# Expert outputs: from a table of rows gathered at the end to weighted rows scattered onto the output with accumulation

## What is computed

```python
# h: (1, 512, 1024); 4 groups of 4 experts, 256 hidden units each
pg_top, g_idx = lax.top_k(p_g, 1)                   # one group for each token
pe_top, e_idx = lax.top_k(p_e, 2)                   # two experts of that group
wts = pg_top * pe_top / sum(pe_top)
combine = sum(one_hot(eid, 16) * wts)
a = einsum('bsd,edf->bsef', h, w_gate)
u = einsum('bsd,edf->bsef', h, w_up)
hid = silu(a) * u * combine
out = x1 + einsum('bsef,efd->bsd', hid, w_down)
```

## Time and profile before

| What | us |
|---|---|
| median of 3 runs | 579.16 |
| lowest and highest run | 576.29, 579.25 |
| the profiled execution, device time | 577.23 |
| its span in the trace | 575.5 |
| PE busy in the span | 498.2 |
| first transposes of expert tile 0 start | 378.0 |
| last product of tile 12 ends | 541.9 |
| last row gathered back lands | 567.8 |

### The profile page before, as it was taken

One profiled execution on the slowest core, in us unless ns is written; L12 is line 12 of the kernel. 1 busy time (PEld: TensorE's weight loads), 2 busy tenths in 40 slices (PEclk: granted clock), 3 DMA queues, 4 the chain that ended last, 5 costly groups with the idle time before them and its releaser, 6 DMA issues.

```text
span 575.5 us, 7543 instructions
## 1 busy us (share of the span) xinstructions
PE 498.2 (87%) x2858; PEld 262.2 (46%) x2858; DVE 232.8 (40%) x591; ACT 112.0 (19%) x273; POOL 134.7 (23%) x150
## 2 busy tenths in 40 slices
PE   5898899999989999999999969369999999999600
PEld 3553544445656676655666655323333333333100
DVE  1127345505697534544455653333421122211133
ACT  2200332233213343313223220300000001000100
POOL 2211388732899100000010211303100000000050
PEclk9999899999998999999999967559999999999955
DMA  8999910006000000470002493636999999970165
GB/s 303 422 386 420 422 56 0 1 1 235 1 1 1 0 1 2 183 329 1 0 1 71 160 354 105 241 110 202 338 419 423 424 425 423 427 303 38 76 235 209
DMA packets 21501, 111.53 MB, mean 194 GB/s; under 512 B 3152, under 2 KB 4688, under 8 KB 16720
## 3 DMA queue, kind: packets, MB, share of 16 engines
q1 hardware_dynamic: 13680, 88.68, 38.5%
q10 hardware_dynamic: 4320, 13.83, 6.1%
q0 software_dynamic: 3456, 8.39, 4.1%
HBM read 81.53 MB, written 33.55 MB: 200 GB/s over the span
## 4 chain that ended last, share of the span: by engine, by line
PE 74%; DVE 7%; issue 4%; DMA 3%; ACT 1%; POOL 1%; POOLq 1%; DVEq 0%; ACTq 0%
PE bank L1416 17%; PE bank L1164 12%; PE bank L1302 10%; PE bank L1437 8%; PE bank L1139 7%; PE bank L1226 5%; PE bank L1240 4%; PE bank L1267 3%; PE bank L1199 3%; PE bank L1401 2%; DMA arena<-expert_rows,small 2%; PE bank L1254 1%; POOL arena L575 1%; PE bank L1424 1%; PE bank L1316 1%
## 5 line engine op out<-in xcount | busy, mean ns | idle before, releaser
L1164 PE MATMUL bank<-arena 128*128 128x512 f32 (+1 forms) x256 | 115.2, 589 | 5.5 <-DVE arena L783 3.1
L1416 PE MATMUL bank<-arena 128*32 128x512 f32 x832 | 96.3, 608 | 1.4 <-DVE arena L1074 0.8
L1139 PE MATMUL bank<-arena 128*128 128x128 f32 (+1 forms) x412 | 61.0, 284 | 20.8 <-DVE arena L865 4.6
L1164 PEld LDWEIGHTS bank<-arena 128*128 128x128 f32 x256 | 49.6, 196 | 61.4 <-issue 54.6
L1139 PEld LDWEIGHTS bank<-arena 128*128 128x128 f32 (+1 forms) x412 | 50.2, 144 | 56.9 <-issue 42.8
L1302 PE MATMUL bank<-arena 128*128 128x512 f32 x128 | 63.5, 624 | 0.0
L1416 PEld LDWEIGHTS bank<-arena 128*32 128x32 f32 x832 | 27.0, 112 | 61.4 <-issue 59.9
L865 DVE COPY arena<-bank 128x512 f32<-128x512 f32 (+2 forms) x64 | 36.2, 586 | 35.7 <-PE bank L1139 35.7
L1437 PE MATMUL bank<-arena 128*32 128x512 f32 x416 | 47.4, 595 | 0.8 <-DVE arena L1090 0.8
L575 POOL DMA_INDIRECT arena<-expert_rows,small x8 | 8.4, 1053 | 144.8 <-issue 144.8
L457 POOL TENSOR_SCALAR small<-small 128x1 f32<-128x1 f32 x16 | 3.7, 232 | 157.5 <-ACT arena L638 95.8
(11 more groups left out here) (148 smaller groups left out, 506.3 us busy)
## 6 DMA issues: line engine op xcount, KB each, us to landing
arena<-in_w_gu SPq DMA_DIRECT2D x17, 2048.0 KB, 13.8
arena<-in_w_dn SPq DMA_DIRECT2D x17, 1024.0 KB, 13.8
slot_rows<-arena SPq DMA_DIRECT2D x1, 11264.0 KB, 36.3
arena<-slot_rows ACTq DMA_DIRECT2D x13, 512.0 KB, 9.5
expert_rows<-arena ACTq DMA_DIRECT2D x13, 512.0 KB, 10.1
expert_rows<-arena SPq DMA_DIRECT2D x1, 4608.0 KB, 45.5
arena<-in_w_out SPq DMA_DIRECT2D x2, 2048.0 KB, 8.2
arena<-in_x SPq DMA_DIRECT2D x4, 512.0 KB, 10.8
```

What stands on the lines that cost most here:

```text
L1139: last = nc.tensor.transpose(TPB[p % 2][0:s.shape[-1], b * P:(b + 1) * P], s, ident)
L1164: last = nc.tensor.matmul(product_bank(i)[:, 0:width], hT[:, k, t * P:(t + 1) * P], w[:, k, :], start=(k == 0), stop=(k == KD - 1))
L1416: last = nc.tensor.matmul(GU[g % 2][BLK * b:BLK * (b + 1), :], xT[g % 2][:, k, BLK * b:BLK * (b + 1)], w_gu[n % RING][:, k, :], start=(k = ...
```

## The change

`expert_rows`, `y_back`, the gathers and the additions on DVE are gone. Instead SP stores x1 to the output (four DMAs, right behind the load of gate and up of the fifth expert in the ring), and each expert tile's rows are added to the output in DRAM by indirect DMAs that accumulate (`compute_op=ALU.add`), issued by POOL (`add`). A tile holds rows of two experts, and a token may have chosen both, so a tile is added in two runs: run 0 takes the rows of the tile's first expert, run 1 those of its second; rows of the other run and empty slots get a row number far out of bounds and are left out. POOL waits for a run to land (`added`) before it issues the run of another expert of the same group. Two runs of the same expert (run 1 of a tile, run 0 of the next) are issued together. Between groups nothing is waited for, as no token has experts of two groups. `y_sb` has three buffers.

The rows must be weighted before they are added. So each slot gets a tag of two numbers, the token's row number and its weight, in a small DRAM table `slot_tags`: filled with the out-of-bounds number early (in place of the fill of `expert_rows`), written by indirect DMAs of 8 bytes a row from POOL beside the rows themselves (eight early ones on the first slots, eight on the final slots), and read back by ACT (`load_tags`, 12 tiles, later the overflow tiles). `left_y` and `right_y` multiply by the weight as they copy. DVE makes the two lists of row numbers from the tags (`tag_rows`). The weights are needed earlier: ACT's exponentials and DVE's `weights_out` move up into the routing of each token tile.

```diff
+        def added_before(g):
+            return 16 * sum(2 if i < ITEMS else 1 for i in range(g % 3, g, 3))
...
-            sp.dma_start(y_dram[(ITEMS + 1) * P:, :].rearrange("(r p) d -> p r d", p=P),
-                         zero.unsqueeze(1).to_broadcast([P, EXTRA - 1, D_MODEL])).then_inc(s_zero, 16)
+            sp.wait_ge(s_fill, 1)
+            sp.dma_start(tag_dram.rearrange("(p r) c -> p (r c)", p=P), tag_fill).then_inc(s_zero, 16)
...
             sp.wait_ge(s_y, len(groups))
             load_gu(4, 4)
+            for t in range(T):
+                sp.wait_ge(s_x1, group["b", t, 1] + 1)
+                sp.dma_start(out[t], x_sb[:, t, :]).then_inc(s_out, 16)
...
-            for t in range(T):
-                sp.wait_ge(s_fin, t + 1)
-                sp.dma_start(out[t], x_sb[:, t, :]).then_inc(s_out, 16)
             sp.wait_ge(s_out, 16 * T)
...
+            def dispatch_tags(t, of, done, rows):
+                for k in range(TOP):
+                    nc.gpsimd.indirect_dma_start(
+                        out=tag_dram, out_offset=bass.IndirectOffsetOnAxis(ap=of[:, t, k:k + 1], axis=0),
+                        in_=tags[:, t, k, :], in_offset=None,
+                        bounds_check=rows * P - 1, oob_is_err=False).then_inc(done, 16)
+
+            def early_tags(t):
+                pool.wait_ge(s_wts, t + 1)
+                dispatch_tags(t, slots[0], s_tagged, ITEMS)
...
             dispatch(0)
             x1_root(2)
+            early_tags(0)
             out_root(1, 3)
             dispatch(1)
+            early_tags(1)
             x1_root(3)
             dispatch(2)
             dispatch(3)
+            early_tags(2)
+            early_tags(3)
...
-            for par in range(2):
-                pool.wait_ge(s_yst[par], 16 * ((LAST + 2 - par) // 2))
+                dispatch_tags(t, slots[1], s_over, TILES)
+
+            pool.wait_ge(s_out, 16 * T)
+
+            def add(g, run):
+                pool.wait_ge(s_ya, g + 1)
+                pool.wait_ge(s_yv, g + 1)
+                pool.wait_ge(s_tok, 1 if g < ITEMS else 2)
+                nc.gpsimd.indirect_dma_start(
+                    out=out_rows, out_offset=bass.IndirectOffsetOnAxis(ap=tag_row[:, run, g:g + 1], axis=0),
+                    in_=y_sb[g % 3], in_offset=None,
+                    bounds_check=SEQ - 1, oob_is_err=False, compute_op=ALU.add).then_inc(s_add[g % 3], 16)
+
+            def added(g, run):
+                pool.wait_ge(s_add[g % 3], added_before(g) + 16 * (run + 1))
+
+            for g in range(0, ITEMS, 3):
+                add(g, 0)
+                added(g, 0)
+                add(g, 1)
+                add(g + 1, 0)
+                added(g, 1)
+                added(g + 1, 0)
+                add(g + 1, 1)
+                add(g + 2, 0)
+                added(g + 1, 1)
+                added(g + 2, 0)
+                add(g + 2, 1)
+            added(LAST - 1, 1)
+            add(LAST, 0)
...
-            for t in range(T):
-                for k in range(TOP):
-                    nc.gpsimd.indirect_dma_start(
-                        out=y_back[t][k], out_offset=None, in_=y_dram,
-                        in_offset=bass.IndirectOffsetOnAxis(ap=slots[2][:, t, k:k + 1], axis=0),
-                        bounds_check=(ITEMS + EXTRA) * P - 1, oob_is_err=False).then_inc(s_back[t], 16)
+            added(LAST, 0)
...
+            act.wait_ge(s_tagged, 16 * TOP * T)
+            load_tags(0, ITEMS)
+
             def left_y(g):
                 act.wait_ge(s_dn, 2 * g + 1)
-                if g >= 2:
-                    act.wait_ge(s_yst[g % 2], 16 * (g // 2))
-                nc.scalar.copy(y_sb[g % 2][:, 0:512], YR[g % 2][0][:, :]).then_inc(s_ya, 1)
+                act.wait_ge(s_tag, 16 if g < ITEMS else 32)
+                if g >= 3:
+                    act.wait_ge(s_add[g % 3], added_before(g))
+                nc.scalar.activation(y_sb[g % 3][:, 0:512], YR[g % 2][0][:, :], ACT.Copy,
+                                     scale=tag_sb[:, g, 1:2]).then_inc(s_ya, 1)
...
                     if g + 3 == LAST:
-                        act.wait_ge(s_over, 16 * TOP * T)
+                        act.wait_ge(s_over, 2 * 16 * TOP * T)
+                        load_tags(ITEMS, TILES)
                     load_x(g + 3)
...
             dve.wait_ge(s_k, 16)
+            for k in range(TOP):
+                link(nc.vector.tensor_copy(tags[:, :, k, 0], konst[:, K_ROW:K_ROW + T]))
...
                 if s in RANKS_AT:
                     ranks_out(RANKS_AT[s])
+                    weights_out(RANKS_AT[s])
...
             ranks_out(2)
+            weights_out(2)
             logits_out(T - 1)
             ranks_out(T - 1)
+            weights_out(T - 1)
...
-            for t in range(T):
-                dve.wait_ge(s_back[t], 32)
-                for k in range(TOP):
-                    ins = nc.vector.scalar_tensor_tensor(x_sb[:, t, :], y_back[t][k], wts[:, t, k:k + 1],
-                                                         x_sb[:, t, :], ALU.mult, ALU.add)
```

More of the change, by code:

```diff
@@ L130, in build @@
         hidT = [at(144, 2, P), at(145, 2, P)]
-        y_sb = [at(110, D_MODEL), at(114, D_MODEL)]
-        y_back = [[at(kb + 4 * i, D_MODEL) for i in (0, 1)] for kb in (16, 24, 48, 56)]
+        y_sb = [at(110, D_MODEL), at(114, D_MODEL), at(136, D_MODEL)]
         route = at(118, T, P)
@@ L166, in build @@
         logits = sm(T, E)
-        wts = sm(T, TOP)
-        slots = [sm(T, TOP).bitcast(i32) for _ in range(3)]
+        tags = sm(T, TOP, 2)
+        tag_fill = sm(2 * TILES)
+        slots = [sm(T, TOP).bitcast(i32) for _ in range(2)]
         slot_f = sm(3, T, TOP)
@@ L955, in weights_out @@
                 link(nc.vector.tensor_tensor(r[:, 77:78], r[:, 76:77], r[:, 72:73], ALU.mult))
[L956 to L957 removed]
+                link(nc.vector.reciprocal(tags[:, t, 0, 1:2], r[:, 77:78]))
+                nc.vector.tensor_tensor(tags[:, t, 1, 1:2], tags[:, t, 0, 1:2], r[:, 74:75], ALU.mult).then_inc(s_wts, 1)
             for t in range(T):
@@ L1094, in right_y, with tag_rows @@
                 dve.wait_ge(s_dn, 2 * g + 2)
-                if g >= 2:
-                    dve.wait_ge(s_yst[g % 2], 16 * (g // 2))
-                nc.vector.tensor_copy(y_sb[g % 2][:, 512:1024], YR[g % 2][1][:, :]).then_inc(s_yv, 1)
+                if g >= 3:
+                    dve.wait_ge(s_add[g % 3], added_before(g))
+                nc.vector.tensor_scalar(y_sb[g % 3][:, 512:1024], YR[g % 2][1][:, :], tag_sb[:, g, 1:2], None,
+                                        ALU.mult).then_inc(s_yv, 1)
+            def tag_rows(lo, hi):
+                dve.wait_ge(s_tag, 16 if lo == 0 else 32)
+                if lo == 0:
+                    for run in range(2):
+                        cut = konst[:, K_CUT + run * ITEMS:K_CUT + (run + 1) * ITEMS]
+                        last = nc.vector.tensor_tensor(tag_row[:, run, lo:hi], tag_sb[:, lo:hi, 0], cut, ALU.add)
+                else:
+                    last = nc.vector.tensor_copy(tag_row[:, 0, lo:hi], tag_sb[:, lo:hi, 0])
+                last.then_inc(s_tok, 1)
             x_read(0)
@@ L1109, in _ @@
                     slots_out()
-                if g == 1:
-                    for t in range(T):
-                        weights_out(t)
+                    tag_rows(0, ITEMS)
+                if g == LAST - 1:
+                    tag_rows(ITEMS, TILES)
             right_y(LAST)
```

56 lines of the change are left out of this document (31 added, 25 removed).

## The result

The change makes the kernel slower. Measured side by side, the changed kernel has a median of 588.18 us (585.62 to 593.72, four runs) and the kernel before 577.72 us (571.99 to 579.25, four): a ratio of 1.025, 95% interval 1.020 to 1.031. The forecast was 559.6 us with a range of 553 to 572. The profiled execution has a span of 585.7 us against 575.5.

A forecast was written before the change was run, and what follows sets the result against it. PE was taken to bound the expert tiles, and a chain of DMAs and additions the end. The span, 575.5 - 21.2 + 0.8 + 0.4 + 0.5 = 556.0 us, became 557.7 device time and a 559.6 us median, range 553 to 572.

The forecast's parts named there:

- The sum: Whole kernel: profiled span of 575.5 us, less 21.2 at the end, plus 0.8, 0.4 and 0.5, giving 556.0 us.
- The expert tiles: Between first and last expert tile: the chain of adds keeps pace with PE's 11.96 us a tile, costing nothing.
- L: Time of one accumulating scatter from semaphore to landing: 5.5 us at the quiet end, near 9 beside weight loads.
- Rival 1: Expert tiles: adds lag while DMA is full, PE loses about 5 us; 565 to 574 us, chance 0.16.
- 7.3 us of cover: Expert tiles: slack between copying hidden values at 491.01 and the down using them at 498.7, allowing a late eviction.
- DMA load and cover: Expert tiles: extra traffic of 3.3 us over eight full tiles, hidden by 9 us of slack in weight loads; nothing.
- The end: Behind tile 11's right half: three scatters in a row, 16.5 us in place of 37.7, a gain of 21.2 us.
- The routing: Before the expert tiles: earlier weights +0.8 us, row-number copies 0.4, x1 stores delaying the last row scatters +0.5.
- Rival 2: Adds slow by themselves even with DMA idle, bounding the kernel from 418 us on; 602 to 604 us, chance 0.12.
- Rival 3: Small gain: scatters of 9 to 11 us everywhere, end 27 to 33 us; 570 to 577 us, chance 0.06.
- Rival 4: Accumulating nearly free: 4.1 us a scatter, end 12.3 us; 555.4 us, chance 0.66 together with the main forecast.

The follow-up runs named there:

- e2: The changed kernel with its 25 scatters onto the output as plain writes, not accumulating; 580.5 us in one run.
- e14: The changed kernel with only the experts' weights loaded in rows of 4 KB; 571.74 us, ratio 0.994 to the kernel before.
- e16: The kernel before with weights in rows of 4 KB and one jump past the overflow passes; 572.81 us, ratio 0.996.
- e3: The changed kernel with POOL waiting for the last row scatters to land before the tag scatters of token tiles 2 and 3; 590.71 us in one run.

## Why the prediction was wrong

**The sum.** It gave a span of 556.0, and 585.7 was measured: 29.7 us more. In the sum's own terms: the start was to cost 1.7 and cost 5.4 (3.7 missing), the tiles 0 and cost 14.8, and from tile 11's right half to the end of the span 37.7 was to become 16.5 and became 27.6 (11.1 missing). Together 29.6.

**The expert tiles: the step that failed.** "I expect L near 9 here, 11 at the median store's landing. Both are under 11.96". A link is issue to landing plus the second issue of the pair and POOL's steps. Landing was 12.4 in the median with 22 for the first, the second issue stands 1.84 us behind the first, and the links came to 13 to 16. I took the 10.3 us store of the earlier trace rows as an upper neighbour because a run has fewer rows. For a plain scatter that was sound: `e2` has 7.5. What failed is the add: I gave it 1.4 us at the quiet end (4.1 to 5.5) and nothing in the full stretch, and there, beside 16 KB rows, it costs 5 to 6 us (12.4 and 13.1 against 7.5), and 2.0 beside rows of 4 KB. The second issue of the pair was not in the sum either. Rival 1 had the mechanism (adds that lag, a start 8 us late, evictions past 7.3 us of cover) and too small a price: 5 us where it took 14.8, from L = 14 that it had named, but with the first link of 22 us and PE's lower clock after each long pause not counted. It also got only 16%. The plain scatter of 11.4 us beside weight loads, on which it stood, comes near the 12.4 measured by luck, since plain scatters of the expert tiles land in 7.5; but as an upper bound for the full stretch it was the row to use: with POOL's 0.8 us it gives a link of 12.2, longer than a tile.

**DMA load and cover.** The cover for weights held: with 4 KB rows, at the same load, PE loses nothing. The load itself came near what was costed: from 415 to 513 us POOL's scatters hold 15.5% of the engines' time in `e14`, and ACT's queue, now without the stores, 10.0% where it has 21.0% in `e16`. That is 4.5% of 98 us more, 4.4 us where 3.3 were costed.

**The end.** L = 5.5 at the quiet end was near: the last issues are 5.9 and 5.5 us apart, and the three links with the second issue of the pair came to 18.8 us for 16.5. The Trainium skill's rule of halved rate (Collectives: The Full Stack, Part 3: Why 7x under link rate) would add 1.25 us to a plain landing, by the prediction's estimate. The measured difference is 2.6, of which 0.6 is POOL's longer issue, so it is more than rate. The sum ended at the last landing, though, and the span doesn't: the drain adds 4.7, and PE's jumps in the first profile 4 more. Before, both lay beside gathers and stores (the drain from 552.2 to 568.8 us), so the chain in the earlier trace rows didn't show them. Taking 37.7 us of chain away asked for "what is late next", and PE's branches up to 570.5 us stood in the trace of before.

**The routing.** `weights_out(1)`, the copies and the shift of the slot numbers came out near what was costed: slot numbers 0.9 us later, 1.2 costed. "They may delay the last row scatters by 0 to 2 us: +0.5" was the miss. The scatters lost 2.1 us in landing, the loads behind them 1.8, and the tag scatters, of which I said that only the DMA engines could mix them, are part of it by `e3`, a single run. I had looked at the stretch up to 370 us with its free 64%, while the stores ran to 375.

**The rivals.** Rival 2 (the add slow by itself) falls: 5 us quiet. Rival 3's end (27 to 33 us) has the measured 27.6 by chance, through drain and jumps. Rival 4 falls: the add is not free.

## What to carry to other kernels

The landing of a small DMA is read from the same kind of DMA in the same company. An accumulating one has no such row in a trace of plain ones, and its price at a quiet end (2.6 us here) says little of its price beside a full stream (5 to 6 us): take the worst row of the trace, put the add on top, and ask first whether the stream could go in rows of 4 KB. A chain that runs once for each tile must be clearly shorter than the tile, with every second issue and wait in it; when it is longer by 2 us, buffers only choose when the loss begins. When the last chain of a kernel is shortened, list what every engine's queue still does behind its last useful instruction, jumps and drains too, since that becomes the end.

## What the runs showed of the hardware

- A taken jump over the code of an overflow tile costs PE 3.0 to 3.7 us in the median and the other engines 0.05; nine of them can end a kernel. Nested, they are one of 3.4 to 3.9 us.
- POOL's last DRAIN takes 4.73 us in the profiles of kernels that end on scatters and wait for the last (14; 4.74 in the two with plain scatters). Where it begins while gathers still run (four profiles), it ends 1.0 us behind the last landing.
- An accumulating scatter takes POOL 1.54 us to issue, a plain one 0.96. Its landing is 2.6 us later at quiet, 2.0 beside weight loads in rows of 4 KB, 5 to 6 beside rows of 16 KB.
- Cutting loads of 2 MB into four with rows of 4 KB left their rate as it was and took 2.7 us off a neighbour's load of 0.5 MB.
- On one of three chips PE lost 12 to 16 us beside a burst of sixteen indirect DMAs, with nothing waited for that the profile shows; the cause is open.
